# Chunk products, transposes and attention scores on 64x64 tiles of TensorE, and modulation units in twos

## The chip, the cores and the metric

The kernel runs on one core of a Trainium2 chip. The metric is the device time of one execution in microseconds (us). The other engines named here are VectorE (DVE), ScalarE (ACT), GpSimd (POOL) and SyncE (SP), which issues the DMAs of the weight stream. All arithmetic in the part that is changed is float32.

## The reference, cut to what matters

Two transformer blocks run one after the other on 256 rows of width 1024; the second one also takes 256 context rows. The change touches the mixer of the first block, which joins two branches, and a small product that the second block needs.

```python
def first_block(x, ...):
    x = x + 0.5 * swiglu(rms_norm(x, ffn1_norm), w1, w3, w2)
    p = rms_norm(x, mix_norm) @ w_in
    y_a = rwkv7_mixer(token_shift(p[..., :SHIFT_COLS], mu), ...) @ rwkv_proj
    y_b = fox_mixer(p[..., SHIFT_COLS:SHIFT_COLS + FOX_COLS], ...) @ fox_proj
    x = x + (gate_a * y_a + gate_b * y_b) @ w_out
    return x + 0.5 * swiglu(rms_norm(x, ffn2_norm), ...)

# RWKV-7: per head of 64, over time, state S (64x64)
S_t = S_{t-1} diag(w_t) + (S_{t-1} a_t) b_t^T + v_t k_t^T;   y_t = S_t r_t

# FoX: softmax attention of 8 heads of 64 with a forget gate
s = q @ k.T * scale + cum[query] - cum[key];   s = where(key <= query, s, -inf)
o = softmax(s) @ v

# second block: modulation rows from the condition vectors c and c_ctx
mod_x = silu(c) @ w_ada + b_ada      # w_ada is 1024 x 9216
mod_c = silu(c_ctx) @ w_ada + b_ada
```

## The kernel before, in words

**Streams and rings.** All weights come as units of 1 MB (128 partitions x 2048 float32) in one fixed order, through a ring of three buffers `RAW`. SP issues the load of a unit when the buffer of the unit three places before is free. Each ordinary unit is split into a high and a low part (ACT at L316, DVE at L324) and multiplied by three products (L329 to L331). The 36 units of `w_ada` are not split: TensorE reads them straight from `RAW` in float32. `ada(n)` (L562) issues n of these products, each 32 output partitions by 512 columns, four to a unit; when the four of a unit are done, its buffer is free. 26 of the 36 units stand in the stream in one piece, between the second and the third unit of the gate weights.

**RWKV in chunks.** The recurrence is done in four chunks of 64 rows, for eight heads: `IT` = 4 tiles of 128 partitions with two heads each, head r on partitions 64r to 64r+63. For a chunk c

- `turn(c, 0, BK)` and `turn(c, 1, AV)` transpose, by products with an identity, the 64x64 blocks of `BK` and `AV`. Per tile i there is one product with all 64 rows of the upper head against 128 columns (L671) and two with 64x64 for the lower head (L673, L674). The results fill banks 0 and 1 of PSUM; ACT copies them out (L1201).
- `products(c)` makes the 64x64 products of keys and decayed queries: per tile i six products of 64x64 (L684 to L687, L690, L691) and one of 64x128 (L688) into banks 2 to 5. DVE masks them (L1685, L1687).
- `ada(4)` follows: one modulation unit.

The emission order is `turn 0, products, turn 1, ada(4)` for each chunk. `turn` waits until ACT has emptied banks 0 and 1 (`tr_out`), `products` until DVE has emptied banks 2 to 5 (`tt_out`). Then eight products per chunk at L711 and L712 follow (the w step), 64x64 each.

**The inverse.** The triangular inverse of each chunk's matrix is made in levels of doubling block size: `z_step(n)` (L765) and `x_step(n)` (L781, L783) for n = 4 to 23, each with products of 64x64 on the diagonal tiles (head 0 on rows and columns 0 to 63 of the array, head 1 on 64 to 127). DVE masks after z (L1719) and adds after x (L1732, L1735). z runs two steps ahead of x.

**FoX beside it.** With k = n - 4, and h = k // 2, the eight attention heads are laid between the steps of the inverse. A pair of steps does, on TensorE:

- k even: x, `scores(h+1)`, z, `turn_probs(h)`, `ada(4)`
- k odd: x, `values(h)`, z, `ada(4)`

`scores(h)` makes three blocks of 128x128 scores: q times k (L723), the cumulative forget gates added by a product with a column of the identity (L725) and, for the two diagonal blocks, the causal mask added by a product with the identity (L728). DVE takes the row maxima (L1692, L1693), ACT the exponentials (L1212), DVE scales them (L1699, L1700). `turn_probs` transposes the three 128x128 blocks (L738) into bank 0, ACT copies them out (L1223), and `values` multiplies by v (L748 to L750) into bank 1. `scores` starts with k up to 12; the last two pairs of steps (k = 16 to 19) have no head at all, only x, z and `ada`.

On DVE the order in a step is: the add of x, the row maxima (k even), the mask of z, the scaling of probabilities (k odd).

After the inverse a chain of state updates runs beside the gate products.

Of the kernel before, what the change touches and what calls it, by code (L numbers as in the profile page):

```python
# [23 lines left out]
ALU = mybir.AluOpType  # L24
# [3 lines left out]
P = 128  # L28
ROWS = 256
# [98 lines left out]
def build(nc, stream, xin, params, consts, lora, bada, rope, dft, iota, out):  # L128
    with ExitStack() as ctx:
# [266 lines left out]
        def _(pe):  # L396
# [268 lines left out]
            def turn(c, n, src):  # L665

                if c or n:
                    pe.wait_ge(S("tr_out"), 2 * c + n)
                eye = con("ident")
                for i in range(IT):  # L670
                    nc.tensor.matmul(BK8[0][:, i * CH:(i + 1) * CH], src[0:CH, i, c].rearrange("p a b -> p (a b)"),  # L671
                                     eye[0:CH, 0:CH], start=True, stop=True)
                    nc.tensor.matmul(BK8[1][0:CH, i * CH:(i + 1) * CH], src[CH:P, i, c, 1], eye[CH:P, CH:P], start=True, stop=True)  # L673
                    last = nc.tensor.matmul(BK8[1][CH:P, i * CH:(i + 1) * CH], src[CH:P, i, c, 0], eye[CH:P, CH:P],  # L674
                                            start=True, stop=True)
                last.then_inc(S("tr"), 1)

            def products(c):

                if c:  # L680
                    pe.wait_ge(S("tt_out"), 2 * c)
                for i in range(IT):
                    o = slice(i * CH, (i + 1) * CH)
                    nc.tensor.matmul(BK8[2][0:CH, o], BK[0:CH, i, c, 0], AR[0:CH, i, c, 0], start=True, stop=True)  # L684
                    nc.tensor.matmul(BK8[2][CH:P, o], BK[CH:P, i, c, 0], AR[CH:P, i, c, 0], start=True, stop=True)
                    nc.tensor.matmul(BK8[3][CH:P, o], BK[0:CH, i, c, 1], AR[0:CH, i, c, 0], start=True, stop=True)
                    nc.tensor.matmul(BK8[3][0:CH, o], BK[CH:P, i, c, 1], AR[CH:P, i, c, 0], start=True, stop=True)  # L687
                    nc.tensor.matmul(BK8[4][:, o], BK[0:CH, i, c].rearrange("p a b -> p (a b)"), AR[0:CH, i, c, 1],  # L688
                                     start=True, stop=True)
                    nc.tensor.matmul(BK8[5][0:CH, o], BK[CH:P, i, c, 1], AR[CH:P, i, c, 1], start=True, stop=True)  # L690
                    last = nc.tensor.matmul(BK8[5][CH:P, o], BK[CH:P, i, c, 0], AR[CH:P, i, c, 1], start=True, stop=True)  # L691
                last.then_inc(S("tt"), 1)

            pe.wait_ge(S("bk_ready"), 1)
# [21 lines left out]
            def scores(h):  # L716

                i, p0 = h // 2, 64 * (h % 2)
                if h:
                    pe.wait_ge(S("fexp"), h)  # L720
                for q, k, mask in ((0, 0, True), (1, 0, False), (1, 1, True)):
                    o = BK8[6][:, (q + k) * P:(q + k + 1) * P]
                    nc.tensor.matmul(o, FQ[p0:p0 + 64, i, q * P:(q + 1) * P], FK[p0:p0 + 64, i, k * P:(k + 1) * P],  # L723
                                     start=True, stop=False)
                    last = nc.tensor.matmul(o, con("ident")[:, h:h + 1].to_broadcast([P, P]), STB[:, k * P:(k + 1) * P],  # L725
                                            start=False, stop=not mask)
                    if mask:
                        last = nc.tensor.matmul(o, con("ident"), con("causal"), start=False, stop=True)  # L728
                last.then_inc(S("scores"), 1)

            def turn_probs(h):
                pe.wait_ge(S("probs"), h + 1)
                if h:
                    pe.wait_ge(S("prt_out"), h)
                else:
                    pe.wait_ge(S("w_out"), 4)
                for q in range(3):
                    last = nc.tensor.transpose(BK8[0][:, q * P:(q + 1) * P], SCO[:, h % 2, q * P:(q + 1) * P], con("ident"))  # L738
                last.then_inc(S("prt"), 1)

            def values(h):
                p0 = 64 * (h % 2)
                pe.wait_ge(S("prt_out"), h + 1)
                if h >= 2:
                    pe.wait_ge(S("fo_out"), h - 1)
                o = BK8[1][p0:p0 + 64, 0:ROWS]
                v = (lambda kt: FV[:, kt, 64 * h:64 * h + 64])
                nc.tensor.matmul(o[:, 0:P], v(0), PRT[:, h % 2, 0:P], start=True, stop=True)  # L748
                nc.tensor.matmul(o[:, P:ROWS], v(0), PRT[:, h % 2, P:2 * P], start=True, stop=False)
                last = nc.tensor.matmul(o[:, P:ROWS], v(1), PRT[:, h % 2, 2 * P:3 * P], start=False, stop=True)  # L750
                last.then_inc(S("fox_o"), 1)
# [43 lines left out]
            for n in range(NC, 6 * NC):  # L795
                k = n - NC
                h = k // 2
                x_step(n)
                if k % 2 == 0 and h + 1 < NH:
                    scores(h + 1)  # L800
                elif k % 2 and h < NH:
                    values(h)
                if n + 2 < 6 * NC:
                    z_step(n + 2)
                if k % 2 == 0 and h < NH:
                    turn_probs(h)
                ada(4)


            def gate(t, half):  # L810
# [216 lines left out]
        def _(act):  # L1027
# [189 lines left out]
            for h in range(NH):  # L1217
                if h + 1 < NH:
                    soft(h + 1)
                act.wait_ge(S("prt"), h + 1)  # L1220
                if h >= 2:
                    act.wait_ge(S("fox_o"), h - 1)
                A(PRT[:, h % 2], BK8[0][:, 0:384], ACT.Copy).then_inc(S("prt_out"), 1)  # L1223
                p0 = 64 * (h % 2)
                act.wait_ge(S("fox_o"), h + 1)
                A(YB[p0:p0 + 64, h // 2], BK8[1][p0:p0 + 64, 0:ROWS], ACT.Copy).then_inc(S("fo_out"), 1)


            act.wait_ge(ada_used, ADA)
# [198 lines left out]
        def _(dve):  # L1428
# [216 lines left out]
            V.tensor_tensor(KK[:], KK[:], pair(2), ALU.mult).then_inc(S("kk_norm"), 1)  # L1645
            dve.wait_ge(S("f_act"), 3)
            link(V.tensor_tensor(F3[:], F3[:], F2[:], ALU.subtract))
            V.tensor_tensor_scan(STB[0:NH], F4[:], F3[:], 0.0, ALU.mult, ALU.add).then_inc(S("lf_cum"), 1)
            split_lo(dve, r0 + 7)

            dve.wait_ge(S("shift_out"), 10)
# [73 lines left out]
            for n in range(NC, 6 * NC):  # L1725
# [8 lines left out]
                else:  # L1734
                    V.tensor_tensor(X2[:, c, 1].rearrange("p i n -> p (i n)"), X2[:, c, 1].rearrange("p i n -> p (i n)"),  # L1735
                                    BK8[4 + n % 2][:, ROWS:512], ALU.add).then_inc(S("x_add"), 1)
                if k % 2 == 0 and h + 1 < NH:
                    row_max(h + 1)
                if n + 2 < 6 * NC:
                    z_mask(n + 2)  # L1740
                if k % 2 and h + 1 < NH:
                    probs(h + 1)

# [392 lines left out]
def _consts():  # L2136
# [19 lines left out]
    same = (r[:, None] // CH == r[None] // CH).astype(np.float32)  # L2156
    put("blk", same)
    put("cen", np.eye(P, dtype=np.float32) - same / CH)
    put("causal", np.where(r[None] <= r[:, None], 0.0, -3.0e38))
    j, g, v = r // MODR, r % MODR // 2, r % 2  # L2160
    put("asel", (g < 9)[:, None] & (2 * (2 * g + j % 2) + v == np.arange(40)[:, None]).T)
    return con
# [38 lines left out]
```

## Time and profile before

| | us |
|---|---|
| median of three runs | 1832.56 |
| lowest and highest run | 1832.21, 1837.78 |
| the profiled execution's own time | 1838.37 |
| its span, first to last instruction | 1836.6 |
| TensorE (PE) busy in it | 1777.0 |
| DVE, ACT busy | 1060.7, 652.4 |

In the profile PE is the matmul side of TensorE and PEld the loading of its stationary operand. A float32 product is done in two passes, and each pass is a record of its own: 16 products make x32. The duration of a PE record holds the depth of the pipeline too, so that records overlap; the time that a product takes of a dense sequence is read from start to start. PEclk is the granted clock, 1.00 for 2.4 GHz and 0.50 for 1.2 GHz. In the timeline a row with x16 or x32 joins several records of the same line.

### The profile page before, as it was taken

To read this page: it belongs to the slowest core of one execution; us is meant where nothing else is said; L and a number is where in the kernel's file an instruction comes from. 1 tells how busy PE (TensorE), PEld (TensorE's weight loads), DVE (VectorE), ACT (ScalarE), POOL (GpSimd) and SP (SyncE) were. 2 spreads that over 40 slices of the span, in tenths; PEclk is the share of its full clock that TensorE was granted. 3 is DMA by queue.
4 is the path that set the end of the run, shared out by engine and by line. 5 is a ranking of instruction groups with operands and counts; after the bars stand their busy time and mean duration, and the time that the engine had idled before them with its cause. 6 is when DMAs were issued, how large, how long until landed. Compare 5 with 4: busy or idle time off the path is not lost.

```text
span 1836.6 us, 31577 instructions
## 1 busy us (share of the span) xinstructions
PE 1777.0 (97%) x13038; PEld 1600.9 (87%) x13038; DVE 1060.7 (58%) x1569; ACT 652.4 (36%) x763; POOL 5.2 (0%) x13
## 2 busy tenths in 40 slices
PE   6999999999999999999999999899999999999997
PEld 6999898666699899998888888788889889989997
DVE  6676747133366767666464554773156733767766
ACT  4333454011244433343212222332236524453332
POOL 0000000000000000000000000000000000000000
PEclk9999999579999999999999999999999999999999
DMA  6555556246524455533222232133223335544451
GB/s 237 190 180 177 209 192 241 69 162 230 214 80 167 166 188 180 180 138 115 91 91 99 84 114 91 69 138 115 92 82 114 100 110 184 184 154 177 176 189 59
DMA packets 37534, 267.69 MB, mean 146 GB/s; under 512 B 4192, under 2 KB 4448, under 8 KB 5456
## 3 DMA queue, kind: packets, MB, share of 16 engines
q1 hardware_dynamic: 36432, 262.37, 39.8%
q0 software_dynamic: 1024, 4.17, 0.6%
q8 instruction: 62, 1.02, 0.2%
q14 instruction: 16, 0.13, 0.0%
HBM read 265.48 MB, written 1.05 MB: 145 GB/s over the span
## 4 chain that ended last, share of the span: by engine, by line
PE 92%; DVE 4%; ACT 2%; issue 1%; DMA 1%; DVEq 0%; POOL 0%; SPq 0%; ACTq 0%
PE PS L329 24%; PE PS L330 23%; PE PS L331 23%; PE PS L542 2%; PE PS L543 2%; PE PS L544 2%; PE PS L562 2%; PE PS L976 2%; PE PS L671 1%; PE PS L407 1%; PE PS L1009 1%; PE PS L996 1%; ACT W_HI L316 1%; PE PS L673 1%; DVE NT L1443 1%
## 5 line engine op out<-in xcount | busy, mean ns | idle before, releaser
L329 PE MATMUL PS<-H_HI,W_HI 128*128 128x256 f32 (+1 forms) x2128 | 653.6, 307 | 21.0 <-DVE H_LO L1454 11.9
L330 PE MATMUL PS<-H_LO,W_HI 128*128 128x256 f32 (+1 forms) x2128 | 649.2, 305 | 0.0
L331 PE MATMUL PS<-H_HI,W_LO 128*128 128x256 f32 (+1 forms) x2128 | 648.8, 305 | 0.0
L316 ACT ACTIVATE W_HI<-RAW 128x2048 fp32r<-128x2048 f32 x213 | 407.2, 1912 | 589.0 <-PE PS L331 557.9
L324 DVE TENSOR_TENSOR W_LO<-RAW,W_HI 128x2048 fp32r<-128x2048 f32 x213 | 487.2, 2288 | 187.2 <-ACT W_HI L316 186.7
L329 PEld LDWEIGHTS PS<-H_HI,W_HI 128*128 128x128 f32 x2128 | 413.0, 194 | 41.2 <-issue 25.0
L330 PEld LDWEIGHTS PS<-H_LO,W_HI 128*128 128x128 f32 x2128 | 413.4, 194 | 15.3 <-issue 0.2
L331 PEld LDWEIGHTS PS<-H_HI,W_LO 128*128 128x128 f32 x2128 | 413.3, 194 | 15.1
L329 PE MATMUL PS<-HID_HI,W_HI 128*128 128x256 f32 (+1 forms) x704 | 218.4, 310 | 3.3 <-DVE XC L1504 3.3
L330 PE MATMUL PS<-HID_LO,W_HI 128*128 128x256 f32 (+1 forms) x704 | 217.9, 309 | 0.0
L331 PE MATMUL PS<-HID_HI,W_LO 128*128 128x256 f32 (+1 forms) x704 | 217.8, 309 | 0.0
L1504 DVE SCALAR_TENSOR_TENSOR XC<-PS,GATE,XC 128x256 f32<-128x256 f32 x264 | 114.5, 478 | 124.8 <-PE PS L331 124.6
L329 PEld LDWEIGHTS PS<-HID_HI,W_HI 128*128 128x128 f32 x704 | 134.3, 191 | 11.1 <-DVE XC L1504 3.9
L331 PEld LDWEIGHTS PS<-HID_HI,W_LO 128*128 128x128 f32 x704 | 134.4, 191 | 6.9
L330 PEld LDWEIGHTS PS<-HID_LO,W_HI 128*128 128x128 f32 x704 | 134.4, 191 | 6.8
L1504 DVE SCALAR_TENSOR_TENSOR XC<-PS,XC 128x256 f32<-128x256 f32 x176 | 68.6, 420 | 62.4 <-PE PS L331 62.4
L1486 DVE TENSOR_TENSOR PROD<-SILU,PS 128x256 f32<-128x256 f32 (+1 forms) x88 | 42.5, 483 | 105.6 <-PE PS L331 101.7
L542 PE MATMUL PS<-W_HI,H_HI 128*128 128x512 f32 x176 | 69.6, 395 | 0.0
L544 PE MATMUL PS<-W_HI,H_LO 128*128 128x512 f32 x176 | 68.5, 389 | 0.0
L543 PE MATMUL PS<-W_LO,H_HI 128*128 128x512 f32 x176 | 68.5, 389 | 0.0
L1062 ACT ACTIVATE SILU<-PS 128x256 f32<-128x256 f32 (+1 forms) x88 | 37.7, 429 | 70.4 <-PE PS L331 70.3
L1493 DVE TENSOR_TENSOR HID_LO<-PROD,HID_HI 128x256 fp32r<-128x256 f32 (+1 forms) x88 | 43.3, 492 | 3.0
(334 smaller groups left out, 1890.0 us busy)
## 6 DMA issues: line engine op xcount, KB each, us to landing
RAW<-stream SPq DMA_DIRECT2D x249, 1024.0 KB, 4.8
XC<-xin SPq DMA_DIRECT2D x2, 512.0 KB, 5.1
XC<-xin POOLq DMA_DIRECT2D x1, 1024.0 KB, 5.2
out<-NT POOLq DMA_DIRECT2D x2, 512.0 KB, 2.9
CON<-consts POOLq DMA_DIRECT2D x1, 548.0 KB, 6.0
LW<-lora POOLq DMA_DIRECT2D x1, 512.0 KB, 6.6
DFT<-dft POOLq DMA_DIRECT2D x1, 512.0 KB, 4.0
ROPE<-rope POOLq DMA_DIRECT2D x1, 256.0 KB, 3.5
```

The costliest lines, as they stand in the source:

```text
L316: nc.scalar.activation(W_HI[s % RING][:], RAW[u % RING][:], ACT.Copy).then_inc(hi_done, 1)
L324: nc.vector.tensor_tensor(W_LO[s % RING][:], RAW[u % RING][:], W_HI[s % RING][:].bitcast(F32), ALU.subtract).then_inc(lo_done, 1)
L329: nc.tensor.matmul(acc, w_hi, x_hi, start=first, stop=False)
L330: nc.tensor.matmul(acc, w_hi, x_lo, start=False, stop=False)
L331: return nc.tensor.matmul(acc, w_lo, x_hi, start=False, stop=last)
L542: nc.tensor.matmul(bank[:], xh, wh, start=st, stop=False)
L543: nc.tensor.matmul(bank[:], xh, wl, start=False, stop=False)
L544: last = nc.tensor.matmul(bank[:], xl, wh, start=False, stop=sp_)
L1062: A(SILU[:, t % 2, 0:n], BK8[2 * (t % 2)][:, 0:n], ACT.Silu).then_inc(S("silu"), 1)
L1486: V.tensor_tensor(PROD[:, t % 2, 0:n], SILU[:, t % 2, 0:n], BK8[2 * (t % 2) + 1][:, 0:n], ALU.mult).then_inc(S("hid_prod"), 1)
L1493: V.tensor_tensor(HID_LO[:, t % 2, 0:n], PROD[:, t % 2, 0:n], HID_HI[:, t % 2, 0:n].bitcast(F32), ALU.subtract).then_inc(S("hid_lo"), 1)
L1504: last = V.scalar_tensor_tensor(out=XC[:, h, m], in0=BK8[4 + m % 4][:, h * ROWS:(h + 1) * ROWS], scalar=gate(h, m), in1=XC[:, h, m], op0=A ...
```

## The change

All products of `turn`, `products`, `scores` and `turn_probs` become products on 64x64 quarters of the array. A pair (r, w) names the quarter: rows r of the array (partitions 64r.. of the operands) and columns w (partitions 64w.. of the output). The quarters are visited in the order (0,0), (0,1), (1,1), (1,0). The products with 128 stationary columns are each cut in two.

- `turn`: 16 products per call, before 12. `products`: 32, before 28.
- `scores`: for query block q = 0 the keys 0 to 127, for q = 1 the keys 0 to 255 in one piece. Per block two products (w = 0, 1) of q times k, two for the forget gates and two for the causal mask: 12 products, all on the 64 rows of the head's half. The constant `causal` is now held twice, on both halves of the partitions, and the upper left 64 columns of the mask are skipped where nothing is masked. The gates are read from the half of `STB` that belongs to the head, so DVE copies its 8 rows to partition 64 on (one more instruction behind the scan at L1648, with a wait between them).
- `turn_probs`: 12 products of 64x64 instead of three transposes of 128x128; the results lie in banks 0 and 1, and ACT's one copy reads both. It also waits for `fo_out` now, since `values` writes to the right half of bank 0 instead of bank 1.
- The order in a pair of steps becomes
  - k even: x, z, `scores(h+1)`, `turn_probs(h)`
  - k odd: x, z, `values(h)`, `ada(8)`

  and on DVE the mask of z goes ahead of the row maxima.

```diff
-                eye = con("ident")
+                eye = con("eye")
                 for i in range(IT):
-                    nc.tensor.matmul(BK8[0][:, i * CH:(i + 1) * CH], src[0:CH, i, c].rearrange("p a b -> p (a b)"),
-                                     eye[0:CH, 0:CH], start=True, stop=True)
-                    nc.tensor.matmul(BK8[1][0:CH, i * CH:(i + 1) * CH], src[CH:P, i, c, 1], eye[CH:P, CH:P], start=True, stop=True)
-                    last = nc.tensor.matmul(BK8[1][CH:P, i * CH:(i + 1) * CH], src[CH:P, i, c, 0], eye[CH:P, CH:P],
-                                            start=True, stop=True)
+                    for r, w in ((0, 0), (0, 1), (1, 1), (1, 0)):
+                        last = nc.tensor.matmul(BK8[r][CH * w:CH * (w + 1), i * CH:(i + 1) * CH], src[CH * r:CH * (r + 1), i, c, (w + r) % 2],
+                                                eye[CH * r:CH * (r + 1)], start=True, stop=True)
...
+                    for a in range(2):
+                        for r, w in ((0, 0), (0, 1), (1, 1), (1, 0)):
+                            rows_, j = slice(CH * r, CH * (r + 1)), (w + r) % 2
+                            bank = 4 + r if a else 2 + j
+                            last = nc.tensor.matmul(BK8[bank][CH * w:CH * (w + 1), i * CH:(i + 1) * CH], BK[rows_, i, c, j],
+                                                    AR[rows_, i, c, a], start=True, stop=True)
...
+                for q, (cols_, last_block) in enumerate(((P, 0), (ROWS, P))):
+                    for w in range(2):
+                        nc.tensor.matmul(BK8[6][CH * w:CH * (w + 1), q * P:q * P + cols_],
+                                         FQ[p0:p0 + CH, i, q * P + CH * w:q * P + CH * (w + 1)], FK[p0:p0 + CH, i, 0:cols_],
+                                         start=True, stop=False)
+                    for w in range(2):
+                        nc.tensor.matmul(BK8[6][CH * w:CH * (w + 1), q * P:q * P + cols_],
+                                         con("eye")[p0:p0 + CH, h:h + 1].to_broadcast([CH, CH]), STB[p0:p0 + CH, 0:cols_],
+                                         start=False, stop=False)
+                    for w in range(2):
+                        o = q * P + last_block + CH * w
+                        last = nc.tensor.matmul(BK8[6][CH * w:CH * (w + 1), o:q * P + cols_], con("eye")[p0:p0 + CH],
+                                                con("causal")[p0:p0 + CH, 0:P - CH * w], start=False, stop=True)
...
                 if h:
                     pe.wait_ge(S("prt_out"), h)
+                    pe.wait_ge(S("fo_out"), h)
...
                 for q in range(3):
-                    last = nc.tensor.transpose(BK8[0][:, q * P:(q + 1) * P], SCO[:, h % 2, q * P:(q + 1) * P], con("ident"))
+                    for r, w in ((0, 0), (0, 1), (1, 1), (1, 0)):
+                        o = q * P + CH * w
+                        last = nc.tensor.matmul(BK8[r][CH * w:CH * (w + 1), q * CH:(q + 1) * CH], SCO[CH * r:CH * (r + 1), h % 2, o:o + CH],
+                                                con("eye")[CH * r:CH * (r + 1)], start=True, stop=True)
...
                 x_step(n)
-                if k % 2 == 0 and h + 1 < NH:
-                    scores(h + 1)
-                elif k % 2 and h < NH:
-                    values(h)
                 if n + 2 < 6 * NC:
                     z_step(n + 2)
                 if k % 2 == 0 and h < NH:
+                    if h + 1 < NH:
+                        scores(h + 1)
                     turn_probs(h)
-                ada(4)
+                if k % 2:
+                    if h < NH:
+                        values(h)
+                    ada(8)
...
-            V.tensor_tensor_scan(STB[0:NH], F4[:], F3[:], 0.0, ALU.mult, ALU.add).then_inc(S("lf_cum"), 1)
+            link(V.tensor_tensor_scan(STB[0:NH], F4[:], F3[:], 0.0, ALU.mult, ALU.add))
+            V.tensor_copy(STB[CH:CH + NH], STB[0:NH]).then_inc(S("lf_cum"), 1)
```

## Rows read from the trace of the kernel before

**Rows 1.** The page: chain by engine (part 4), stream loads (part 6).

```profile
PE 92%; DVE 4%; ACT 2%; issue 1%; DMA 1%; DVEq 0%; POOL 0%; SPq 0%; ACTq 0%
...
RAW<-stream SPq DMA_DIRECT2D x249, 1024.0 KB, 4.8
```

**Rows 2.** Windows: stretch, length, busy PE, PEld, DVE, ACT, POOL; PEclk, DMA share, GB/s.

```profile
324.90:383.20 58.30, 58.30 (x442) 40.61 (x441) 6.38 (x9) 4.78 (x8) 0.53 (x1) 0.50 0.16 56
383.20:386.30 3.10, 3.10 (x62) 3.10 (x60) 0.00 (x0) 0.99 (x3) 0.00 (x0) 0.50 0.81 325
...
396.40:464.20 67.80, 67.80 (x959) 46.74 (x959) 24.46 (x64) 11.72 (x42) 0.00 (x0) 1.00 0.63 226
464.20:480.50 16.30, 14.23 (x255) 8.23 (x253) 4.89 (x11) 0.87 (x2) 0.00 (x0) 1.00 0.90 330
495.50:498.90 3.40, 3.40 (x23) 3.18 (x24) 0.00 (x0) 0.29 (x1) 0.00 (x0) 0.53 0.01 2
```

**Rows 3.** Timeline of PE, chunk stage: start, duration, engine, line, work [idle before].

```profile
324.05 0.40 PE L671 MATMUL PS<-CON,BK 64*128 64x64 f32 x2 [1.52 <-DVE BO L1679]
...
327.66 0.68 PE L688 MATMUL PS<-AR,BK 64*128 64x64 f32 x2
328.28 0.36 PE L690 MATMUL PS<-AR,BK 64*64 64x64 f32 x1
...
328.29 0.36 PE L684 MATMUL PS<-AR,BK 64*64 64x64 f32 x1
...
328.44 0.31 PE L690 MATMUL PS<-AR,BK 64*64 64x64 f32 x1
...
328.54 0.31 PE L687 MATMUL PS<-AR,BK 64*64 64x64 f32 x1
...
332.38 0.68 PE L671 MATMUL PS<-CON,AV 64*128 64x64 f32 x2
...
333.40 0.68 PE L671 MATMUL PS<-CON,AV 64*128 64x64 f32 x2
...
336.46 1.93 PE L562 MATMUL PS<-RAW,SCZ 128*32 128x512 f32 x8
```

**Rows 4.** Timeline of DVE and of ACT in the first chunk.

```profile
332.57 0.69 DVE L1685 TENSOR_TENSOR TTNK<-PS,CON 128x512 f32<-128x512 f32 x1 [8.78 <-PE PS L691]
...
336.58 0.60 ACT L1201 ACTIVATE AVR<-PS 128x512 f32<-128x512 f32 x1 [8.42 <-PE PS L674]
```

**Rows 5.** Timeline of PE and ACT, one pair of steps of the inverse.

```profile
419.85 0.68 PE L765 MATMUL PS<-X,TTNK 64*64 64x64 f32 x16
...
420.46 0.55 PE L738 MATMUL PS<-CON,SCO 128*128 128x128 f32 x3
...
421.42 0.49 ACT L1223 ACTIVATE PRT<-PS 128x384 f32<-128x384 f32 x1
...
423.06 0.43 PE L748 MATMUL PS<-PRT,FV 128*64 128x128 f32 x2
...
423.86 0.68 PE L765 MATMUL PS<-X,TTNK 64*64 64x64 f32 x16
...
424.47 1.06 PE L562 MATMUL PS<-RAW,SCZ 128*32 128x512 f32 x8
...
425.47 0.34 PE L781 MATMUL PS<-ZM,X 64*64 64x64 f32 x4
...
426.59 0.49 PE L723 MATMUL PS<-FK,FQ 64*128 64x128 f32 x2
...
429.54 0.68 PE L765 MATMUL PS<-X,TTNK 64*64 64x64 f32 x16
```

**Rows 6.** Timeline of PE, from the last head's pair to the end.

```profile
464.22 0.34 PE L781 MATMUL PS<-ZM,X 64*64 64x64 f32 x4
...
465.20 0.68 PE L765 MATMUL PS<-X,TTNK 64*64 64x64 f32 x16
...
479.40 1.06 PE L562 MATMUL PS<-RAW,SCZ 128*32 128x512 f32 x8 [1.55 <-DMA RAW<-stream]
```

More of the change, by code:

```diff
@@ L682, in products @@
                 for i in range(IT):
[L683 to L691, printed above, removed]
+                    for a in range(2):
[4 more added lines that the diff above has]
+                                                    AR[rows_, i, c, a], start=True, stop=True)
                 last.then_inc(S("tt"), 1)
@@ L720, in scores @@
                     pe.wait_ge(S("fexp"), h)
[L721 to L728, printed above, removed]
+                for q, (cols_, last_block) in enumerate(((P, 0), (ROWS, P))):
[11 more added lines that the diff above has]
+                                                con("causal")[p0:p0 + CH, 0:P - CH * w], start=False, stop=True)
                 last.then_inc(S("scores"), 1)
@@ L743, in values @@
                 pe.wait_ge(S("prt_out"), h + 1)
-                if h >= 2:
-                    pe.wait_ge(S("fo_out"), h - 1)
-                o = BK8[1][p0:p0 + 64, 0:ROWS]
+                o = BK8[0][p0:p0 + 64, ROWS:2 * ROWS]
                 v = (lambda kt: FV[:, kt, 64 * h:64 * h + 64])
@@ L1222, in _ @@
                     act.wait_ge(S("fox_o"), h - 1)
-                A(PRT[:, h % 2], BK8[0][:, 0:384], ACT.Copy).then_inc(S("prt_out"), 1)
+                A(PRT[:, h % 2].rearrange("p (r b q) -> p b r q", r=3, b=2), PS[:, 0:2, 0:3 * CH].rearrange("p b (r q) -> p b r q", r=3), ACT.Copy).then_inc(S("prt_out"), 1)
                 p0 = 64 * (h % 2)
                 act.wait_ge(S("fox_o"), h + 1)
-                A(YB[p0:p0 + 64, h // 2], BK8[1][p0:p0 + 64, 0:ROWS], ACT.Copy).then_inc(S("fo_out"), 1)
+                A(YB[p0:p0 + 64, h // 2], BK8[0][p0:p0 + 64, ROWS:2 * ROWS], ACT.Copy).then_inc(S("fo_out"), 1)
             act.wait_ge(ada_used, ADA)
@@ L1736, in _ @@
                                     BK8[4 + n % 2][:, ROWS:512], ALU.add).then_inc(S("x_add"), 1)
+                if n + 2 < 6 * NC:
+                    z_mask(n + 2)
                 if k % 2 == 0 and h + 1 < NH:
                     row_max(h + 1)
-                if n + 2 < 6 * NC:
-                    z_mask(n + 2)
                 if k % 2 and h + 1 < NH:
@@ L2158, in _consts @@
     put("cen", np.eye(P, dtype=np.float32) - same / CH)
-    put("causal", np.where(r[None] <= r[:, None], 0.0, -3.0e38))
+    put("causal", both(np.where(r[None] <= r[:CH, None], 0.0, -3.0e38)))
     j, g, v = r // MODR, r % MODR // 2, r % 2
```

## The prediction

> **What bounds the kernel now.** I read the page's chain of waits first: 92% of what ended last is TensorE's own work, ACT and the DMA have 2% and 1% [rows 1]. So time taken out of a dense TensorE stage reaches the end, and the question in each stage is what is late next. Then the windows, for the clock. From 324.9 to 383.2, the chunk stage, TensorE is busy all of the 58.3 us and is granted half of its clock, 1.2 GHz (PEclk 0.50). The inverse, 396.4 to 464.2, is just as busy at the full 2.4 GHz, while the stream brings 226 GB/s; behind it, to 480.5, TensorE idles 2 us and the DMA share is 0.90 [rows 2]. The timeline of the chunk stage shows why a stage that is always busy is not dense: L688 has 128 stationary columns, its two records start at 327.66, and the next product waits until 328.28. 0.62 us go where the streaming of 64 columns twice would need 0.2. Between quarters of 64x64, on the other hand, there is no such gap: L690 and L684 start 0.01 us apart, the second pass follows at 328.44, and the next product of the same quarter at 328.54, 0.10 later [rows 3]. What this case shows of the clock: it fell with the sparse chunk stage (behind 1.5 us of waiting for DVE) and came back only behind the w step, 62 records in 3.1 us, two side by side each 0.10 us [rows 2, 3].
>
> **The chunk stage.** It lasts from 324.05 to the window that starts at 383.20: 59.15 us, four times 14.8 and a start. In a chunk now: `turn` 4 x 1.02 (332.38 to 333.40), twice; `ada(4)` 1.9 at this clock; the rest, some 4.9, is `products` [rows 3]. After the change every product is on a quarter of 64x64, four quarters make a round, and nothing switches the shape but `ada`. A `turn` is 4 rounds, `products` 8, so 64 rounds in all.
> A round of four quarters alone does not stand in the trace. Lower bound: two passes as long as a pass of two quarters. At full clock an x step of 32 records, 16 passes, takes 0.98 us (464.22 to 465.20) [rows 6], 0.061 a pass, so 0.122 a round; at half clock 2 x 0.10 = 0.21. Upper bound: four quarters take twice as long as two, 0.24 at full clock. I take the lower, since the rows at 328.28 to 328.54 have all four quarters in flight and the pass still takes 0.10 [rows 3].
> A chunk at full clock: 0.49 + 0.98 + 0.49 + 1.00 for `ada(4)` with its two switches (424.47 to 425.47) [rows 5] = 2.96. Four: 11.8, and 0.2 for the first start.
> The clock: the 1.5 us wait ahead of the stage stays, so I expect it to fall there once. Another fall, at 495.5, lasted 3.4 us and ended in dense products [rows 2]; such a stretch costs 1.7 us. Stage 13.7 us, gain 45.4. With no fall it is 47.1; with the clock low all through, a chunk is 0.85 + 1.70 + 0.85 + 1.9 = 5.3, the stage 21.2 and the gain 38.
> What is late next here: ACT's copy, 0.60, plus some 0.15 before and after, lies between turn 0 and turn 1, under 0.98 of `products`, and later under `ada`; DVE's two masks of 0.69 lie under turn, `ada` and turn, 2 us [rows 4]. `ada` needs a unit per 3 us where it needed one per 15. Three units lie in the ring at the start; the fourth is asked for when the first is used, at about 328.5, lands 4.8 later [rows 1] and is needed at about 337. No wait, but margins of 0.1 to 3 us where there were 8.
> A rule speaks against `products`. The rows: in the w step the two records come from different row halves, write one bank, and a pass is 0.10 us, what one quarter's pass takes [rows 2, 3]. The Trainium skill (TensorEngine Tiling, Gotcha 1: PSUM Pressure) says that different row tiles cannot access the same bank at the same time. By it the first 16 rounds of `products`, where both row halves write banks 2 and 3, would take 2.0 us more in all; the sum goes by the rows, which do not show it.
>
> **The w step and the first scores.** At half clock the w step takes 3.4 (62 of 64 records in 3.10) [rows 2]; at full clock 32 x 0.061 = 1.95. Gain 1.4, nothing if the clock stays low. `scores`: 2.95 now (426.59 to 429.54) [rows 5]. After: a pass of 128 columns at full clock takes as long as one of 64 at half, 0.10 to 0.11. Block q = 0 has three pairs of products, two passes each: 6 x 0.11; q = 1 has 4 x 0.22 and 2 x 0.11. Sum 1.76, both columns side by side as L690 shows with its partner. Gain 1.2 for `scores(0)`. The first z steps behind it follow DVE and stay.
>
> **The pairs of steps in the inverse.** Now [rows 5]: x 1.12, scores 2.95, z 0.61, turned probabilities 0.47 (ahead of 1.00 for `ada` to the next x at 421.93), `ada` 1.00; x 1.13, values 0.80, z 0.61, `ada` 1.00. Sum 9.69. After: z right behind x is without a switch, 8 passes, 0.49, and x in front of it 0.98 [rows 6]. x 0.98, z 0.49, scores 1.76, probabilities 3 rounds 0.37, x 0.98, z 0.61, values 0.80, `ada(8)` 1.00 + 0.88 = 1.88. Sum 7.87.
> The moved parts bring a wait nearer. ACT copies the turned probabilities only after the softmax of the head ahead: from the end of scores (419.85) to the end of the copy (421.91) it takes 2.06 us, with the signal 2.15 [rows 5]. TensorE has 0.37 + 0.98 + 0.61 = 1.96 in between, and scores ends 0.12 earlier without its switch. So `values` waits 0.3 (0 to 0.5), and z, `ada` and all of the stream stand behind it: 8.17 a pair. The new wait of `turn_probs` on `fo_out` and the wait on `probs` lie behind a whole `ada(8)`, x and z, 3 us and more; nothing. DVE's new order costs nothing, it has 24.5 / 7 = 3.5 us of work in a pair [rows 2]. Seven pairs have scores: 7 x (9.69 - 8.17) = 10.6. Bounds 8 to 13.
>
> **The tail.** From 464.22 to the end of the last `ada`, 480.4, 16.2 us [rows 6]. TensorE's own work falls to about 13 by the parts above, but the last `ada` already waits 1.55 for the stream at a DMA share of 0.90 [rows 2, 6]. The last three pairs use six units. In twos, the buffers come free later: the last unit is asked for when the unit three ahead is used, and takes 4.8 us [rows 1], or 1.5 to 2 more with another ahead of it in the queue (an estimate: half of a unit's 2.9 us at 367 GB/s, up to two thirds). Worked through, the last `ada` ends 14.8 to 16.5 us after the pair begins. Gain 0.5.
> **DVE's copy** in front (8 x 256, the nearest row is a mask of 128 x 512 with 0.69 us [rows 4]) lies in a part where TensorE waits for DVE only once, at the end, for `BO` [rows 3], which itself stands behind a product of TensorE. That wait takes the delay up. I take nothing; 0.7 slower at most.
>
> **The sum.** 45.4 + 1.4 + 1.2 + 10.6 + 0.5 = 59.1 us. The profiled execution took 1838.4, 1.8 outside its span, and would take 1779.3. It is 5.8 above the median; against the median of the runs, 1832.6, the forecast is 1773.5.
>
> **The rivals.**
> *Issue-bound rounds (15%).* At full clock a pass of two quarters takes 0.061, a little more than half of 0.10 to 0.107 at half clock, so something beside the columns is in it. If that is a time per record, four quarters take 0.24 a round: 88 rounds (64, and 24 for the probabilities) x 0.122 = 10.7 us of the gain. Gain 48.4, time 1784.2. For it: no stretch has four quarters at full clock. Against it: at 328.28 two records start 0.01 apart. The Trainium skill (TensorE: Matmul & The Clock Gate, Back-to-back issue gap) has a floor of about 25 ns for a product of up to 64 columns; two records in 0.061 agree with that as well as with streaming.
> *The clock stays low (11%)* through chunks and w step, because the stage is short and each `ada` and wait breaks it. Gain 59.1 - 7.5 - 1.4 = 50.2, time 1782.4. Against it: w step and gate products brought it back within 3.4 us of dense work [rows 2].
> *The inverse gains nothing (8%)*: softmax chain and stream take back what scores gives, a pair stays near 9.7. Gain 48.5, time 1784. For it: the chain of ACT is as long as TensorE's work beside it. Against it: a pair's two units, 2.1 MB, need 5.7 us at the 367 GB/s that the stream has at full share (330 / 0.90) [rows 2], and the pair lasts 8.
> *Slower (3%): quarters of a round do not run side by side*, each product drains like L688. 88 rounds x 4 x 0.62 = 218 us for 10.7: 1832.6 - 59.1 + 207 = 1981. It decides from a round of 0.122 + 59.1 / 88 = 0.79 us, 0.20 a product. The starts of L690 and L684 speak against it [rows 3].
> *No change (1%)*: only if something not seen holds the stages' ends.
>
> **Chances and range.** The forecast has 62%, with its own range from 1767 (no fall of the clock, no wait of `values`) to 1780. With the cases at 1782 to 1784 and some mixtures the range is 1765 to 1789. Within 0.3% (5.5 us) this kernel cannot be told from no change. Faster 96%, same 1%, slower 3%.
>
> **What would show it.** In the profile after: the stage from the first `turn` to the w step 12 to 15 us long; PEclk 0.50 for one window of some 3 us and then 1.00; starts of the same line 0.12 us apart per round. The pair of steps 8.2 us from `ada` to `ada`, scores 1.8, and a wait of L748 to L750's product on ACT's `PRT` of some 0.3. A wait of L562 on the stream of 2 to 5 us at the end of the inverse. Wrong it would be with rounds near 0.24, with PEclk at 0.50 past the second chunk, or with waits on `RAW` in the chunks.

## The result, and the profile after

| | before | after |
|---|---|---|
| median of the runs, us | 1835.1 (4 runs) | 1787.8 (4 runs) |
| the profiled execution, us | 1838.4 | 1788.0 |
| its span | 1836.6 | 1786.2 |

The ratio is 0.9736, interval 0.9706 to 0.9765: 47 us less. In a second comparison, with four other executions, it is 0.9719 (0.9689 to 0.9749). One execution of the changed kernel took 3398 us, nothing on record shows why, and it is left out of the ratio (without it the median is 1787.6).

The forecast, 1773.5 with 1765 to 1789, had the sign and the place, and held the time at its edge: of 59.1 us of gain, 50.4 stand between the two profiles. The median lies 14.3 us above the forecast: 8.7 of it are the gain that is missing, 5.8 the step from the profiled execution to a median of three runs, which the fourth run and the profile after did not bear out. The forecast's own range ended at 1780; only the part that was added for the rivals and mixtures of them reached the result, and none of these rivals came true. The page after:

```profile
span 1786.2 us, 32228 instructions
...
PE 1718.9 (96%) x13366; PEld 1564.9 (88%) x13366; DVE 1059.5 (59%) x1570; ACT 652.2 (37%) x763; POOL 5.1 (0%) x13
...
PE 91%; DVE 4%; ACT 2%; issue 2%; DMA 1%; DVEq 0%; POOL 0%; SPq 0%; ACTq 0%
```

TensorE still makes up the chain as in [rows 1], but "issue" went from 1% to 2%: time in which it waited for nothing that the profile knows. The windows of the stages, in the columns of [rows 2]:

```profile
325.50:336.60 11.10, 8.51 (x400) 6.45 (x400) 2.90 (x5) 2.98 (x5) 0.00 (x0) 1.00 0.57 213
336.60:340.00 3.40, 3.40 (x71) 1.72 (x68) 0.96 (x2) 0.92 (x2) 0.00 (x0) 0.50 0.24 34
...
342.16:345.75 3.59, 2.33 (x70) 2.09 (x68) 1.22 (x1) 1.15 (x3) 0.00 (x0) 1.00 0.91 338
354.24:411.18 56.94, 54.41 (x1163) 41.65 (x1163) 23.43 (x64) 11.70 (x42) 0.00 (x0) 1.00 0.68 258
411.18:428.66 17.48, 13.28 (x274) 7.90 (x271) 4.58 (x10) 0.87 (x2) 0.00 (x0) 1.00 0.99 364
```

The chunk stage runs at the full clock but for 3.4 us from 336.60 on, the third chunk's `ada` and the start of the fourth chunk. The timeline of PE in that stage answers to [rows 3]:

```profile
325.50 0.69 PE L672 MATMUL PS<-CON,BK 64*64 64x64 f32 x32 [1.52 <-DVE BO L1684]
325.99 1.14 PE L685 MATMUL PS<-AR,BK 64*64 64x64 f32 x64
326.92 0.68 PE L672 MATMUL PS<-CON,AV 64*64 64x64 f32 x32
327.53 1.06 PE L562 MATMUL PS<-RAW,SCZ 128*32 128x512 f32 x8
328.53 0.69 PE L672 MATMUL PS<-CON,BK 64*64 64x64 f32 x32
...
332.12 0.69 PE L672 MATMUL PS<-CON,BK 64*64 64x64 f32 x32
332.64 0.76 PE L685 MATMUL PS<-AR,BK 64*64 64x64 f32 x40
335.64 0.52 PE L685 MATMUL PS<-AR,BK 64*64 64x64 f32 x21 [2.24 <-issue]
...
336.62 1.93 PE L562 MATMUL PS<-RAW,SCZ 128*32 128x512 f32 x8
```

The first chunk is as forecast: `turn` 0.49 for 4 rounds, `products` 0.93 for 8, `ada` 1.00, 3.03 in all. In the third chunk `products` stops after 40 of its 64 records, in the middle of a call that has no wait, for 2.24 us. Behind it the clock is low (`ada` 1.9 instead of 1.0). One pair of steps and the end of the inverse answer to [rows 5, 6]:

```profile
385.40 1.92 PE L562 MATMUL PS<-RAW,SCZ 128*32 128x512 f32 x16
387.25 0.34 PE L783 MATMUL PS<-ZM,X 64*64 64x64 f32 x4
...
392.53 0.43 PE L750 MATMUL PS<-PRT,FV 128*64 128x128 f32 x2 [0.34 <-ACT PRT L1227]
...
393.33 1.92 PE L562 MATMUL PS<-RAW,SCZ 128*32 128x512 f32 x16
...
421.62 1.06 PE L562 MATMUL PS<-RAW,SCZ 128*32 128x512 f32 x8 [1.37 <-DMA RAW<-stream]
...
427.67 1.07 PE L562 MATMUL PS<-RAW,SCZ 128*32 128x512 f32 x8 [1.43 <-DMA RAW<-stream]
```

From `ada` to `ada` 7.93 us, `values` waits 0.34 for ACT, and the last units wait for the stream. Stage by stage, in the two profiled executions:

| stage, us | before | forecast | after |
|---|---|---|---|
| all ahead of the first `turn` | 324.05 | 324.05 | 325.50 |
| chunks | 59.2 | 13.7 | 16.7 |
| w step | 3.5 | 1.95 | 3.4 |
| `scores(0)` | 2.95 | 1.76 | 1.57 |
| first z steps, to the first x | 6.8 | 6.8 | 7.1 |
| seven pairs with scores | 67.8 | 57.2 | 56.9 |
| from the last head's pair to the end of the inverse | 16.2 | 15.7 | 17.5 |
| all behind it | 1356.2 | 1356.2 | 1357.5 |

### The profile page after: what moved, and what is told of

Its sections match the earlier page's. It is cut to its first block, busy times and chain, and to the rows that moved or that the text cites. A ratio compares the mean times of both kernels' runs of the same rounds, so it can differ in the third digit from the quotient of the medians.

```text
span 1786.2 us, 32228 instructions
## 1 busy us (share of the span) xinstructions
PE 1718.9 (96%) x13366; PEld 1564.9 (88%) x13366; DVE 1059.5 (59%) x1570; ACT 652.2 (37%) x763; POOL 5.1 (0%) x13
## 4 chain that ended last, share of the span: by engine, by line
PE 91%; DVE 4%; ACT 2%; issue 2%; DMA 1%; DVEq 0%; POOL 0%; SPq 0%; ACTq 0%
PE PS L329 24%; PE PS L331 24%; PE PS L330 24%; PE PS L542 2%; PE PS L544 2%; PE PS L543 2%; PE PS L562 2%; PE PS L980 2%; PE PS L407 1%; ACT W_HI L316 1%; PE PS L1013 1%; PE PS L1000 1%; DVE NT L1447 1%; DVE NT L1450 1%; DVE W_LO L324 1%
## 5 line engine op out<-in xcount | busy, mean ns | idle before, releaser
L329 PE MATMUL PS<-H_HI,W_HI 128*128 128x256 f32 (+1 forms) x2128 | 653.0, 307 | 21.2 <-DVE H_LO L1458 11.9
L329 PEld LDWEIGHTS PS<-H_HI,W_HI 128*128 128x128 f32 x2128 | 412.5, 194 | 41.7 <-issue 25.0
L329 PE MATMUL PS<-HID_HI,W_HI 128*128 128x256 f32 (+1 forms) x704 | 218.4, 310 | 3.3 <-DVE XC L1508 3.3
L329 PEld LDWEIGHTS PS<-HID_HI,W_HI 128*128 128x128 f32 x704 | 134.3, 191 | 11.2 <-DVE XC L1508 3.9
```

The source lines that it names most:

```text
L329: nc.tensor.matmul(acc, w_hi, x_hi, start=first, stop=False)
```

## The experiments

Eleven kernels ran, all edits of the changed kernel, and the changed kernel itself once more. Each time is a median of four or five runs, of two in experiments 2 and 3, and the ratio is to the kernel before on the same chip; 1 and 4, 7 and 8 ran on one chip, 5, 9, 10 and 12 on a second, 2, 3, 6 and 11 on a third, and between chips only the ratios compare.

**1. Chunk part undone** (`turn` and `products` as before).

> The changed kernel with `turn` and `products` of the chunk stage as they were before; all else changed. Theory: the drain at each change of shape (0.6 us each) and the half clock that goes with so sparse a stage are what the change removed there, 42.5 of the 50.4 us between the two profiles, and the w step behind it runs at half clock again (1.5 us more). So the chunk stage lasts 59 us again at PEclk 0.50, the pair of steps stays at 8.1 us, and the time is 1788 + 44 = 1832 (1828 to 1835). Rival: the clock fell before only because of what else stood around it, and with the rest changed the old products run at full clock: stage about 35 us, time about 1808.

1827.4 us, ratio 0.9940 (0.9915 to 0.9964). The chunk stage lasts 59.17 us at the low clock, as before, the pair 8.0. So the first theory holds, with a time 0.6 us below its range; by the two ratios of the changed kernel, 37 to 41 us hang on this part alone.

**2. Only `turn` undone, 3. only `products` undone** (the functions of before put back one at a time).

> The changed kernel with turn in its old shapes, products in rounds of four. Theory: a stage needs most of it dense to be granted the full clock; turn has 8 of the chunk's 15 us before and switches shape at every tile, so the clock stays at 0.50 through the stage: a chunk lasts 4.08 x 2 + 1.7 + 1.9 = 11.8 us, the stage 47. Rival: the clock is decided by each piece for itself, comes back in products and ada, and a chunk lasts about 8: stage 32 us.

> The changed kernel with products in their old shapes, turn in rounds of four. Theory: products are the denser part of before (4 pairs of passes in 1.23 us a tile), turn and ada are dense, so the clock comes back after one low stretch: products 8 x 0.35 = 2.8 us at full clock, a chunk 4.9, the stage 20 to 23 us. Rival: any part with switches keeps the clock low: products 4.9, turn 0.85 twice, ada 1.9, a chunk 8.5 and the stage 34 us.

With the old `turn` 1814.6 us, ratio 0.9883 (0.9861 to 0.9905); with the old `products` 1787.0, ratio 0.9732 (0.9714 to 0.9751). Windows inside the chunk stage, first of the kernel with the old `turn`:

```profile
326.00:370.00 44.00, 44.00 (x472) 31.17 (x468) 6.38 (x9) 4.78 (x8) 0.51 (x1) 0.50 0.20 73
```

and of the one with the old `products`:

```profile
324.00:343.00 19.00, 19.00 (x490) 13.90 (x483) 4.53 (x8) 4.37 (x8) 0.00 (x0) 1.00 0.48 171
```

The stages last 46.5 and 20.2 us, 47 and 20 to 23 by the theory. The same old `products` that took 4.9 us a chunk before run at full clock once `turn` is dense, and the new ones at half clock if it is not. Of the 42.5 us that the stage gave, 39.0 come with `turn`'s shapes alone; the new shapes of `products` alone give 12.7, and are worth 3.5 once `turn` is new. The two do not add up, since they share the clock. And the kernel with the old `products` can't be told from the changed one: its stage is 3.5 us longer, but has no hole and no low stretch, and the w step takes 2.0 instead of 3.4.

**4. The same products without rounds.**

```diff
-                for i in range(IT):
-                    for r, w in ((0, 0), (0, 1), (1, 1), (1, 0)):
+                for r, w in ((0, 0), (0, 1), (1, 1), (1, 0)):
+                    for i in range(IT):
```

> The changed kernel with the loops of turn and products exchanged: the same 64x64 products, but all of one quarter of the array, then all of the next, so there is no round of four. Theory: quarters run side by side only if they are neighbours in the order; one after the other a pass of 64 columns takes 0.06 us alone at full clock, so turn takes 16 x 2 x 0.06 = 1.9 us, products 3.8, a chunk 8.7 and the stage 35 us at full clock: time about 1788 + 18 = 1806, more if the clock falls too. Rival: only the drain at the change of shape mattered, and TensorE itself finds quarters that are free: stage about 17 us, time 1788.

1794.0 us, ratio 0.9758 (0.9730 to 0.9785). The window of the chunk stage:

```profile
325.20:351.60 26.40, 26.40 (x544) 22.86 (x544) 5.79 (x9) 4.78 (x8) 0.53 (x1) 1.00 0.35 131
```

26.5 us at full clock: 9.8 longer than with rounds, not 18. The products overlap somewhat without rounds: 64 products, 128 records, take 5.6 us a chunk, where 128 passes of 0.053 one after the other are 6.8 and rounds need 1.9. Against four chunks like the first one of the changed kernel (3.03 us) the stage is 14.4 longer; there is no hole and no low stretch, which gives 4.6 of it back.

**5. Stream held back in the chunks.**

```diff
+                if j is None and u == RAW_OF[("a", 13)]:
+                    sp.wait_ge(S("tr"), 8)
...
-                ada(4)
+                if c < 3:
+                    ada(4)
...
-            ada(8)
+            ada(12)
```

> The changed kernel, with the load of the fourth modulation unit of the chunk stage (and so all of the stream behind it) held back until the last turn is done; its four products move from the end of the chunk stage to behind the first four z steps, ada(12) there. Theory: TensorE's gaps without a wait (0.35 and 2.24 us inside products, 1.15 in the w step) are a want of instructions, which are fetched by the same DMA engines that the stream fills; in rounds of four TensorE uses them up faster than ever. With the stream quiet during the chunks these gaps go there, the stage lasts 11 to 12 us instead of 16.7 (one ada(4) less, and no fall of the clock behind the gap), but the units come late for ada(12): 5 to 8 us of waiting there, so the time is 1787 to 1792. Rival: a round of four needs instructions faster than they can come at all; the gap of 2.2 us stays with a quiet stream.

1784.4 us, ratio 0.9727 (0.9702 to 0.9752). PE in the chunks:

```profile
328.04 0.40 PE L687 MATMUL PS<-AR,BK 64*64 64x64 f32 x13 [0.20 <-issue]
...
331.77 0.52 PE L687 MATMUL PS<-AR,BK 64*64 64x64 f32 x21 [0.60 <-issue]
...
335.50 0.64 PE L687 MATMUL PS<-AR,BK 64*64 64x64 f32 x29 [0.60 <-issue]
```

Both theories were half right. With a DMA share of 0.07 instead of 0.57 the hole of 2.24 us shrinks to 0.60, so the stream makes it long; but 0.6 a chunk stays with a quiet stream, so the round itself outruns something. The clock stays at 1.00. The stage lasts 13.95 us, not 11 to 12: 1.4 are the holes, and 0.71 are a wait of the w step for ACT's copy, which `ada(4)` covered. The waits for the late units are 3.0 us instead of 5 to 8.

**6. Half as many instructions for the same columns.** The two products of a quarter that share their stationary block are joined.

```diff
-                    for a in range(2):
...
-                            last = nc.tensor.matmul(BK8[bank][CH * w:CH * (w + 1), i * CH:(i + 1) * CH], BK[rows_, i, c, j],
-                                                    AR[rows_, i, c, a], start=True, stop=True)
+                        last = nc.tensor.matmul(BK8[2 + j][CH * w:CH * (w + 1), i * P:(i + 1) * P], BK[rows_, i, c, j],
+                                                AR[rows_, i, c].rearrange("p a b -> p (a b)"), start=True, stop=True)
```

> The changed kernel, with the two products of a quarter that share their stationary block (a = 0 and a = 1) joined to one with 128 moving columns: products(c) has 16 products instead of 32 and streams the same columns; DVE masks from banks 2 and 3 in four instructions instead of two. Theory: TensorE gets its instructions more slowly than rounds of four with 64 columns use them up (a hole of 0.6 us a chunk even with a quiet stream, 2.2 with a busy one). With half of the instructions and weight loads in products the holes of 0.35 and 2.2 us go or shrink to under 0.5 in sum, the clock does not fall behind them, and the stage lasts 12 to 13.5 us instead of 16.5; DVE's longer masks (2.0 us) may cost 0.1 to 0.3 a chunk. Time 3 us below the changed kernel's. Rival: the holes come from the weight loads or the banks that four quarters share at once; as there are still four quarters in flight, 2 us of holes stay and the stage lasts 16.

1781.3 us, ratio 0.9703 (0.9688 to 0.9717). Its PE timeline:

```profile
327.98 0.69 PE L672 MATMUL PS<-CON,BK 64*64 64x64 f32 x32
328.77 1.10 PE L683 MATMUL PS<-AR,BK 64*64 64x128 f32 x32
...
331.27 0.69 PE L672 MATMUL PS<-CON,BK 64*64 64x64 f32 x32
```

No hole in any chunk nor in the w step (2.0 us), 12.89 us for the stage, clock 1.00 throughout, the stream as busy as before (share 0.67). Four quarters are in flight as ever, and half the instructions and weight loads take the holes away. `products` now waits 0.3 for DVE's longer masks (327.98 to 328.77 for a `turn` of 0.49). The gain shows in the stage; as a time it is not clear of noise, since the ratio's interval meets both of the changed kernel's.

**7. Old shapes for the attention heads, new order.**

> The changed kernel with scores, turned probabilities and values in their old shapes and banks, but in the new order of the steps and with ada in eights. Theory: the shapes of scores give 1.2 us of a pair and their switches 0.4, the order and ada(8) the small rest; so a pair lasts 9.3 to 9.5 us and not 8.1, the wait of values on ACT's copy of the turned probabilities stays, the first scores cost 1.2 more: time 1788 + 10 = 1798. Rival: the order and ada(8) carry the gain of the pairs: a pair of 8.5 us, time 1791.

1794.0 us, ratio 0.9762 (0.9734 to 0.9791). The pair lasts 9.30 us, `scores(0)` 2.95; `values` waits for `PRT`, but only 0.12 us of TensorE's time. The shapes carry 1.2 of the 1.55 us that a pair gained; the rest came with the order and `ada(8)`.

**8. New shapes, old order of the steps.**

> The changed kernel with the old order in the steps on TensorE (x, scores or values, z, turned probabilities, one modulation unit of ada in every step). Theory: ada in every step costs two more switches a pair, values no longer waits (it has ada and x ahead of it), and at the end of the inverse buffers come free earlier, so a pair lasts 8.1 to 8.3 us, no wait of L750's product on PRT, and the waits on the stream at the end are 2 us and not 4.2: time within 2 us of the changed kernel's, 1786 to 1790. Rival: the order is what makes the pairs short: a pair of 8.8 or more, time 1793.

1785.0 us, ratio 0.9712 (0.9685 to 0.9739). Pairs of 8.0 to 8.16, no wait for `PRT`, one wait for the stream of 2.3 at the end, and 12.3 us from the last `values` to the end of the inverse, where the changed kernel has 14.1 and the kernel before 12.0. With the new shapes the new order gives nothing, and its twos cost about 2 us at the end. Its profile has a second low stretch of the clock, as that of experiment 12 has, and the time is no longer in spite of it.

**9. `ada(8)` ahead of `values`, 10. the same, and `ada(4)` in the last three pairs.**

```diff
                 if k % 2:
+                    ada(8)
                     if h < NH:
                         values(h)
-                    ada(8)
```

> The changed kernel with ada(8) ahead of values in the odd step. Theory: values waits 0.3 us in six pairs for ACT's copy of the turned probabilities; with 1.85 us of ada ahead of it the wait is gone, the number of switches is the same, so the pair lasts 7.85 us instead of 8.13 and the time falls by 2 us. Rival: the wait is paid elsewhere (turned probabilities then wait for values' copy, or the stream): pair and time unchanged.

> As the kernel with ada(8) ahead of values, and in the last three pairs (k = 14 and up) ada(4) in each step. Theory: in twos the buffers of the ring come free later, and the stream, which sets the end of the inverse, ends later: three waits of 1.4 us, 17.5 us from the last head's pair to the end where it was 16.2 before. With one unit a step it is 15 to 16: 1.5 to 2.5 us less than with ada(8). Rival: the stream's rate alone sets the end, the order of use does not matter: no difference.

1781.9 us (0.9717, 0.9687 to 0.9747) and 1784.4 (0.9717, 0.9695 to 0.9739): not to be told from the changed kernel. In their traces the wait for `PRT` is gone, but the pairs last 7.5 to 8.7 us. The long one is this, of the first of the two kernels:

```profile
373.12 2.99 PE L562 MATMUL PS<-RAW,SCZ 128*32 128x512 f32 x16
```

`ada(8)` takes 2.9 instead of 1.85 before `values` starts at 376.04, although no wait is named. Its second unit is not late: a first product reads it at 374.00, the next one starts at 375.05. That is 1.4 us behind the landing of an instruction packet (372.62 to 373.61), as with the holes in the chunks (see below). That was not in my theory. Time from the last `values` to the end, `ada` included, is 10.8 with twos and 10.3 with single units, a gain of 0.6 where I expected 1.5 to 2.5.

**11. Joined products, and one unit of `ada` in every step, ahead of `values`.**

```diff
-                if k % 2:
-                    if h < NH:
-                        values(h)
-                    ada(8)
+                ada(4)
+                if k % 2 and h < NH:
+                    values(h)
```

> As the kernel with joined products, and in the inverse one unit of ada in every step, in the odd step ahead of values. Theory: besides the 3 us of the joined products, values does not wait (ada and z lie ahead of it) and a buffer of the ring comes free in every step, so that pairs last 7.9 us evenly, where ada(8) ahead of values gave 7.5 to 8.6 with waits for the second unit, and the end after the last values is 10 to 11 us instead of 14. Time 5 to 6 us below the changed kernel's, near 1780. Rival: the pairs are bound by the stream (8.0 us for two units), so that only the joined products show: 1783.

1777.2 us, ratio 0.9680 (0.9666 to 0.9693). All five runs lie below all of the kernel with joined products alone, on the same chip. Its pairs last 7.9 to 8.0 evenly, as forecast, and the inverse 73.5 us, against 74.4 in the changed kernel and 75.6 in the one with joined products alone. Of the 3.9 us between these two profiles, though, 2.9 lie ahead of the first `turn` (322.05 against 324.96), in code that is the same: no low stretch of the clock stands there in this profile. So 4 us is what was measured, and 2 of them are what the edit explains.

**12. The changed kernel once more.**

> The changed kernel itself once more, for the comparison on the same chip: ratio 0.973 to before, gaps without a wait at the same places, and the fall of the clock either at the same place or not.

1786.6 us, ratio 0.9719 (0.9689 to 0.9749). The holes are at the same places (0.29, 1.97 and 1.42 us). The clock falls behind the hole of 1.97 us as it did behind that of 2.24, for 3.4 us, and a second time behind that of 1.42, for 10.2 us. The first `turn` starts at 323.72 instead of 325.50 (mean granted clock from 200 us to there 0.99, against 0.97 in the other execution). The windows:

```profile
334.20:337.60 3.40, 3.40 (x73) 1.62 (x64) 1.25 (x2) 0.60 (x1) 0.00 (x0) 0.50 0.14 58
...
344.40:354.60 10.20, 9.64 (x100) 6.13 (x98) 5.53 (x14) 1.04 (x5) 0.00 (x0) 0.50 0.27 93
```

In the second stretch `scores(0)` takes 2.4 instead of 1.57 us and the first z steps, with 0.56 us of waiting for DVE, 9.6 instead of 7.1. The trace of experiment 8 has both stretches too, behind holes of 2.24 and 1.44 us; the changed kernel's first profile, with a last hole of 1.15, has one. So the first fall repeats, the second does not, and some 3 us go with it.

## Why the prediction was right or wrong

**The round** was right (but see the chunk stage for what feeds it): 0.49 / 4 = 0.122 us for `turn`, 0.93 / 8 = 0.116 for `products`, against 0.122. So four quarters run side by side at full clock. Both rules that spoke against it fall by that row. Banks 2 and 3 are written from both row halves in half of `products`, and its rounds are no longer than `turn`'s; the Trainium skill (TensorEngine Tiling, Gotcha 1: PSUM Pressure) would have had them cost more. And 8 records in 0.122 are 0.015 us each, below the floor of 25 ns a product of the Trainium skill (TensorE: Matmul & The Clock Gate, Back-to-back issue gap), which at most holds within one quarter.

**The clock** was right in its effect, wrong in its place. I took one low stretch at the start, behind the wait of 1.5 us. It stayed away there, behind the same wait of 1.52; one came behind the 2.24 us hole, and cost much the same (some 1.6). That this term fits is luck. Experiments 2 and 3 show that the low clock hung on `turn`: the old `products` do not bring it down when `turn` is dense.

How much of the old stage the clock was is an estimate. At full clock a tile of the old `turn` took 0.59 us (324.05 to 324.64 in the trace of before), and the old `products` took 2.9 a chunk (experiment 3). Four chunks of 8 x 0.59 + 2.9 + 1.0 are 34.5 us. By that the clock was some 25 of the 42.5 us, and denser products the other 18.

**The chunk stage**, 13.7 against 16.7, is the term that was mis-sized, by 3.0 us: 2.6 of it are the two holes (0.35 and 2.24). In the working they are missing because I took the round's time for the whole cost and asked only which engine or unit is late next, not what feeds TensorE itself. The w step has the same fault, with a hole of 1.15 us of the 1.45 that it missed. The rival of issue-bound rounds had the right suspect with the wrong form: it gave 1784.2 and came nearer by number, but no round is stretched. TensorE runs at full rate until it has used up what it had, then stands still. That it is instructions that it lacks, the experiments make likely: the holes have no wait in the profile, they go with half the instructions (6), or at half the rate of use (4), and shrink with a quiet stream (5). The traces bear it out. The page counts the packets of a DMA queue named "instruction", 65 of 16 KB each in the changed kernel:

```profile
q8 instruction: 65, 1.06, 0.2%
```

The times of these packets, beside the holes:

| kernel | hole ends, us | matmul records since the first `turn` | packet, start to end | from its end to the hole's |
|---|---|---|---|---|
| changed | 330.27 | 216 | 327.65 to 328.87 | 1.40 |
| changed | 335.64 | 344 | 333.29 to 334.24 | 1.40 |
| changed | 345.44 | 598 | 342.96 to 343.86 | 1.58 |
| 5, stream held | 328.04 | 216 | 325.41 to 326.64 | 1.40 |
| 5, stream held | 331.77 | 344 | 329.18 to 330.49 | 1.28 |
| 5, stream held | 335.50 | 472 | 332.81 to 333.98 | 1.52 |

The holes stand 128 records apart or a multiple of it (two records are missing in the third row), in the middle of a round or not, and each ends 1.3 to 1.6 us behind a packet. With the stream quiet the next packet starts 1.1 us after a hole has ended, and 128 records come every 3.73 us (328.04, 331.77, 335.50). With the stream busy it started 3.0 us after (330.27 to 333.29); a unit of the stream moved in between. A chunk in rounds wants 136 records in 3.03 us, more than this supply gives; joined, 104 in 3.29, or 128 in 4.05; quarter by quarter, 136 in 6.6. The last two fit, and have no hole. That the packets hold TensorE's instructions is read from this match, no view names the engine. The holes of 0.4 to 1.6 us near the first x steps fit the same count (in the changed kernel at record 852, twice 128 behind the 598), but have not been tested apart.

**`scores`** was 0.2 us dearer in the working (1.76) than in the trace (1.57). The rest of a pair came out, the wait of `values` of 0.3 included (0.26 and 0.34 in turn): 56.9 us for seven pairs, 57.2 forecast. Experiment 7 gives this to the shapes, 1.2 us a pair; 8 gives nothing to the order once the shapes are new.

**The tail** was forecast to gain 0.5 and lost 1.3. The mechanism was the stated one, buffers that come free in twos, but I placed the price at the middle of its range, 14.8 to 16.5, and it is 17.5, beyond the end. From issue to landing a unit takes a median of 7.3 us in the inverse after, 4.9 before (the first line is of before, the second of after):

```profile
DMA to landing us min/median/max: 4.7/4.9/8.0
```

```profile
DMA to landing us min/median/max: 4.8/7.3/8.6
```

I had worked with 4.8 and up to 2 more. Loads asked for in twos, within 1 us of each other, are the later ones: with single units at the same pace (experiment 8) the median is 5.4.

**Outside the stages** 2.7 us were lost (1.45 ahead, 1.3 behind), in code that did not change. It is the clock, not the change: ahead of the stage it was low for 3.4 us before and for 6.8 us after, and the second costs up to 1.7 more (the first window is of before, the second of after):

```profile
253.20:256.60 3.40, 3.40 (x19) 3.40 (x18) 1.89 (x1) 3.37 (x4) 0.00 (x0) 0.52 0.02 5
```

```profile
251.30:258.10 6.80, 6.80 (x34) 6.80 (x34) 2.55 (x2) 4.08 (x5) 0.00 (x0) 0.50 0.25 104
```

In experiment 12, with 3.4 us again, the part ahead is 0.3 shorter than before. Behind the stages the clock is low for 27 us in all before and for 31 after. The copy on DVE cost nothing, as forecast: it takes 0.29 us at 292.9, and the 1.45 us are there before it (the products of L329 behind the same L592 start at 280.16 before and 281.62 after) and are the same 1.45 at the first `turn` (324.05 and 325.50).

## What to carry to other kernels

Where a stage is always busy and yet at half clock, look for small products of changing shape: making them one shape gave 42.5 us here, by the estimate above some 25 through the clock and 18 through denser products. The order in rounds alone is 9.8 of them (experiment 4). After such a step, count instructions: two blocks that share a stationary operand belong in one product, and here that join took 3.8 us from the stage, where the new shapes of `products` had taken 3.5. And do not take units from a ring of three in twos; it leaves the average alone and makes the last ones late.

## What was not expected of the hardware

- Rounds of four quarters with 64 float32 columns stood still every 128 matmul records (or a multiple) without a wait, until 1.3 to 1.6 us after an instruction packet had landed: 2.24 us with the stream busy, 0.60 with it quiet, not at all with 128 columns a product.
- Products ordered quarter by quarter still overlapped: 128 records of 64 columns in 5.6 us, 0.044 each, less than the 0.053 that their columns need at full clock if one follows the other (half of the 0.107 at half clock).
- The clock stayed at 1.00 through 2.24 us of standing still and fell to 0.50 only behind it, at 336.6, for 3.4 us. In a second execution of the same program it fell at the same place and once more, at 344.4, for 10.2 us.
